# Two conformer layers and a hybrid block on one core: tile 3's output product and norm moved into the attention loop, four low weight parts subtracted by GpSimd, and other PSUM banks for the conv tiles

## What is computed

```
proj = h @ w_in[l]                       # a, g, zc, q, k, v, za, qi, ki, wi
y_conv = silu(LN(dwconv31(a * sigmoid(g)) + b)) * silu(zc)
score  = sum over 8 heads of relu(qi @ ki^T) * wi;  keep the top 132 keys of each query
y_attn = softmax(q @ k^T over the kept keys) @ v * silu(za)       # 8 heads of 64
h = LN(ALPHA * h + concat(y_conv, y_attn) @ w_out[l])
```

```
z = rmsnorm(x) @ w_in                    # q, k, v, gate_a, u, v_in, gate_b, g_merge
attention of 8 heads over 2 key/value heads, and a gated MLP that mixes positions
y = g0 * (attn @ w_proj_attn) + g1 * (gm @ w_proj_gmlp);  out = rmsnorm(x + y @ w_out)
```

## Time and profile before

| what | value |
|---|---|
| median of three runs | 1045.86 us |
| the profiled execution, its own time | 1047.51 us |
| its span on the core | 1045.7 us |
| TensorE matmul busy | 993.5 us (95%), 6452 instructions |
| VectorE busy | 653.0 us (62%) |
| ScalarE busy | 582.4 us (56%) |
| GpSimd busy | 198.7 us (19%) |
| DMA moved | 152.35 MB, mean 146 GB/s |

### The profile page before, as it was taken

One profiled execution on the slowest core, in us unless ns is written; L12 is line 12 of the kernel. 1 busy time (PEld: TensorE's weight loads), 2 busy tenths in 40 slices (PEclk: granted clock), 3 DMA queues, 4 the chain that ended last, 5 costly groups with the idle time before them and its releaser, 6 DMA issues.

```text
span 1045.7 us, 16515 instructions
## 1 busy us (share of the span) xinstructions
PE 993.5 (95%) x6452; PEld 838.9 (80%) x6452; DVE 653.0 (62%) x1423; ACT 582.4 (56%) x948; POOL 198.7 (19%) x238
## 2 busy tenths in 40 slices
PE   6999999998999899999999899899999899999997
PEld 6998988885577799898888676787888778878885
DVE  3899999876573489999987554637522333332422
ACT  6585881657444458588165834644656565554331
POOL 0100771113120210067111311224200000000001
PEclk9999999998999999999999899999999999999999
DMA  8776874844203768477474521857777535466662
GB/s 294 184 181 172 213 182 122 185 98 122 41 1 94 182 160 192 122 175 187 122 181 102 160 56 41 217 146 182 181 196 211 117 81 139 104 147 135 170 152 81
DMA packets 23820, 152.35 MB, mean 146 GB/s; under 512 B 2864, under 2 KB 3376, under 8 KB 6848
## 3 DMA queue, kind: packets, MB, share of 16 engines
q0 software_dynamic: 9648, 68.75, 35.4%
q1 hardware_dynamic: 14096, 82.55, 22.1%
HBM read 149.20 MB, written 2.10 MB: 145 GB/s over the span
## 4 chain that ended last, share of the span: by engine, by line
PE 79%; ACT 10%; DVE 5%; DMA 4%; issue 2%; POOL 0%; POOLq 0%; SPq 0%; DVEq 0%; ACTq 0%
PE psum_B L1274 20%; PE psum_A L1274 15%; PE psum_A L1307 8%; PE psum_B L1307 8%; PE psum_A L1456 5%; DMA w_lo<-in_weights 3%; PE psum_C L1349 2%; PE psum_A L1667 2%; PE psum_B L1667 2%; ACT w_hi L640 2%; PE psum_B L1410 2%; ACT w_lo L641 2%; PE psum_B L1456 2%; ACT exps L761 1%; DMA w_raw<-in_weights 1%
## 5 line engine op out<-in xcount | busy, mean ns | idle before, releaser
L1752 DVE SCALAR_TENSOR_TENSOR conv_acc<-u,vec,conv_acc 128x528 f32<-128x528 f32 (+1 forms) x240 | 172.4, 756 | 3.2
L1073 POOL DMA_DIRECT2D w_lo<-in_weights x67 | 59.3, 886 | 577.2 <-ACT w_lo L641 551.0
L1274 PE MATMUL psum_B<-x_hi,w_hi 128*128 128x264 f32 (+3 forms) x480 | 134.8, 321 | 5.3 <-DVE mlp_lo L2199 3.6
L640 ACT ACTIVATE w_hi<-w_raw 128x2048 fp32r<-128x2048 f32 (+2 forms) x87 | 129.8, 1493 | 12.7 <-DMA w_raw<-in_weights 12.2
L1274 PE MATMUL psum_B<-x_lo,w_hi 128*128 128x264 f32 (+3 forms) x480 | 132.6, 317 | 0.0
L1274 PE MATMUL psum_B<-x_hi,w_lo 128*128 128x264 f32 (+3 forms) x480 | 132.2, 316 | 0.0
L641 ACT ACTIVATE w_lo<-w_raw 128x2048 fp32r<-128x2048 f32 (+2 forms) x87 | 129.2, 1485 | 0.0
L1274 PE MATMUL psum_A<-x_hi,w_hi 128*128 128x264 f32 (+2 forms) x528 | 125.4, 291 | 3.4 <-DMA w_lo<-in_weights 2.2
L1274 PE MATMUL psum_A<-x_hi,w_lo 128*128 128x264 f32 (+2 forms) x528 | 122.7, 287 | 0.0
L1274 PE MATMUL psum_A<-x_lo,w_hi 128*128 128x264 f32 (+2 forms) x528 | 122.7, 286 | 0.0
L1274 PEld LDWEIGHTS psum_A<-x_hi,w_hi 128*128 128x128 f32 x528 | 87.5, 188 | 7.5 <-issue 5.6
(11 more groups left out here) (362 smaller groups left out, 2120.1 us busy)
## 6 DMA issues: line engine op xcount, KB each, us to landing
w_raw<-in_weights SPq DMA_DIRECT2D x67, 1024.0 KB, 5.3
w_lo<-in_weights POOLq DMA_DIRECT2D x65, 1024.0 KB, 8.4
x_first<-in_x_t SPq DMA_DIRECT2D x4, 528.0 KB, 7.1
h<-in_x SPq DMA_DIRECT2D x1, 2048.0 KB, 10.8
out<-h SPq DMA_DIRECT2D x4, 512.0 KB, 2.6
post_ln_g<-in_post_ln_g SPq DMA_DIRECT2D x2, 512.0 KB, 8.7
post_ln_b<-in_post_ln_b SPq DMA_DIRECT2D x2, 512.0 KB, 10.6
w_raw<-in_weights SPq DMA_DIRECT2D x2, 288.0 KB, 5.4
```

The lines of the kernel that those rows point to most:

```text
L640: act.activation(whi[n % RING][:, a:b], raw[n % RING][:, a:b], ACT.Copy)
L1073: pool.dma_start(wlo[n % RING][:, 0:width], io["weights"][n, :, 0:width], accum_op=ALU.add) \
L1274: mm = pe.matmul(ps[0:cols, i, 0:b - a], w[wp][:, kt, at:at + cols], x[xp][:, kt, a:b], start=(kt == 0 and wp + xp == 0), stop=(kt == KD - ...
L1752: got = dve.scalar_tensor_tensor(dst, src, w, dst, ALU.mult, ALU.add)
```

## The change

It does five things.

- Tile 3's second output half joins the first in both loops (`OUTPUT_AT`: items 34 and 36 in layer 0, 26 and 28 in layer 1). Its norm follows in the loop (`POST_AT`), tile 2's norm in layer 0 moves from item 34 to 32, and tile 4's conv halves are now made at item 38 (30) and behind the loop. Tile 3's rows are turned ahead of tile 4's last half.
- The low parts of the first two blocks behind each layer (`LO_BY_POOL`) are made by GpSimd: raw minus high part, in two halves of 1024 columns (`subtract_hi`), with a signal of its own, `pool_lo`. ScalarE writes only the high part of these.
- Conv tiles keep one bank for both turns and go round D, B, C. The affine step leaves `bank_holders` and stands behind the pair's second copy, directly ahead of its tanh.
- Rows that are turned use banks D and C; layer 0's second output product moves from bank B to A.
- The block's queries are made in halves over the four tiles (`query_half`), key/value and query products in single bank halves; tile 4's rows are turned behind the third key/value product.

```diff
 CONV_AT = {
-    0: ((0, 8, "D", "C"), (1, 10, "B", "C"), (2, 12, "D", "C"), (3, 14, "B", "C"), (4, 16, "D", "C")),
-    1: ((1, 8, "D", "C"), (2, 10, "B", "C"), (3, 12, "D", "C"), (4, 14, "B", "C")),
+    0: ((0, 8, "D"), (1, 10, "B"), (2, 12, "C"), (3, 14, "D"), (4, 16, "B")),
+    1: ((1, 8, "D"), (2, 10, "B"), (3, 12, "C"), (4, 14, "D")),
...
 OUTPUT_AT = {
-    0: ((17, 0, 0, "A"), (19, 0, 1, "B"), (22, 1, 0, "A"), (25, 1, 1, "B"), (27, 0, 2, "A"), (29, 1, 2, "A"),
-        (35, 0, 3, "A")),
-    1: ((17, 0, 1, "A"), (19, 0, 2, "B"), (21, 1, 1, "A"), (23, 1, 2, "A"), (27, 0, 3, "A")),
+    0: ((17, 0, 0, "A"), (19, 0, 1, "A"), (22, 1, 0, "A"), (25, 1, 1, "B"), (27, 0, 2, "A"), (29, 1, 2, "A"),
+        (34, 0, 3, "A"), (36, 1, 3, "A")),
+    1: ((17, 0, 1, "A"), (19, 0, 2, "B"), (21, 1, 1, "A"), (23, 1, 2, "A"), (26, 0, 3, "A"), (28, 1, 3, "A")),
...
 META_AT = ((14, "attn"), (14, "conv"))
-POST_AT = {0: ((0, 26), (1, 28), (2, 34)), 1: ((1, 22), (2, 26))}
-
-OUTPUT_CONV_AT = {0: (37, 39), 1: (29, 31)}
-OUTPUT_BANK = (("A", 1), ("C", 0))
-
-
-INPUT_BANK = {0: ("D", "B", "D", "D", "C"), 1: (None, "D", "B", "D", "C")}
+POST_AT = {0: ((0, 26), (1, 28), (2, 32), (3, 38)), 1: ((1, 22), (2, 26), (3, 30))}
+
+OUTPUT_CONV_AT = {0: 38, 1: 30}
+OUTPUT_BANK = (("A", 1), ("B", 1))
+
+
+INPUT_BANK = {0: ("D", "C", "D", "C", "D"), 1: (None, "D", "C", "D", "C")}
+
+
+KV_AND_Q = (("kv", 0), ("kv", 1), ("kv", 2), ("q", 0, 0), ("kv", 3), ("q", 1, 0), ("q", 2, 0), ("q", 3, 0),
+            ("q", 0, 1), ("q", 1, 1), ("q", 2, 1), ("q", 3, 1))
+KV_BANK = (("A", 0), ("B", 0), ("A", 1), ("B", 1))
+Q_BANK = (("A", 0), ("B", 0), ("A", 1), ("D", 0))
+
+LO_BY_POOL = {NUMBER[key] for key in ((1, "a", 0), (1, "g", 0), (2, "kv", 0), (2, "q", 0))}
...
                     act.activation(whi[n][:, a:b], raw[n][:, a:b], ACT.Copy).then_inc(hi_made.mark(("w", n)), 1)
+                    return
+                if n in LO_BY_POOL:
+                    for half in range(2):
+                        a, b = half * BLOCK // 2, (half + 1) * BLOCK // 2
+                        act.activation(whi[n % RING][:, a:b], raw[n % RING][:, a:b], ACT.Copy) \
+                            .then_inc(hi_made.mark(("w", n, half)), 1)
...
+                            conv_affine(l, op[1])
                             conv_tanh(l, op[1])
                         elif op[0] == "hi":
                             y_hi(l, *op[1:])
-                def bank_holders(i):
+                def gates(i):
                     for op in todo[i]:
                         if op[0] in ("za", "zc"):
                             gate_tanh(l, *op)
-                        elif op[0] == "affine":
-                            conv_affine(l, op[1])
                 for i in range(0, n, 2):
                     take_probs_t(l, i)
                     if i + 2 < n:
...
                         exps(l, i + 3)
-                    bank_holders(i)
+                    gates(i)
                     take_probs_t(l, i + 1)
                     woven(i)
-                    bank_holders(i + 1)
+                    gates(i + 1)
                     woven(i + 1)
                 after = NUMBER[(l + 1, "a" if l < DEPTH - 1 else "kv", 0)]
-                split_hi(after, 0)
                 y_hi(l, "attn", 4)
-                split_hi(after, 1)
+                split_hi(after)
                 if l < DEPTH - 1:
                     x_hi(l, 0)
-                x_hi(l, 1)
-                x_hi(l, 2)
-                split_hi(after + 1)
-                if l < DEPTH - 1:
+                    x_hi(l, 1)
+                    x_hi(l, 2)
+                    split_hi(after + 1)
                     x_hi(l, 3)
+                    split_hi(after + 2)
                     x_hi(l, 4)
+                else:
+                    x_hi(l, 1)
+                    x_hi(l, 2)
+                    split_hi(after + 1)
+                    x_hi(l, 3)
                     split_hi(after + 2)
-                else:
-                    squares(3, square)
-                    split_hi(after + 2)
+                    squares(4, square)
...
-                if (name, t) == ("kv", 1):
-                    x_hi(DEPTH - 1, 3)
-                    squares(4, square)
-                elif (name, t) == ("kv", 2):
+            for t in range(4):
+                take_rows("kv", t)
+                if t == 2:
                     x_hi(DEPTH - 1, 4)
                     split_hi(NUMBER[(2, "vin", 0)])
-                elif name == "q":
-                    next_blocks((2, "q", t))
+            split_hi(NUMBER[(2, "vin", 1)])
+            for t in range(4):
+                take_rows("q", t)
...
         def _(pool):
+            def subtract_hi(n):
+
+                for half in range(2):
+                    a, b = half * BLOCK // 2, (half + 1) * BLOCK // 2
+                    pool.wait_ge(hi_made.sem, hi_made.at(("w", n, half)))
+                    pool.tensor_tensor(wlo[n % RING][:, a:b], raw[n % RING][:, a:b], whi[n % RING][:, a:b].bitcast(F32),
+                                       ALU.subtract).then_inc(pool_lo.mark((n, half)), 1)
+
...
-                split_lo(after)
-                if l < DEPTH - 1:
-                    ln_deviation((l, "post", 3), 3, P)
-                    split_lo(after + 1)
-                    ln_deviation((l, "post", 4), 4, P)
-                    split_lo(after + 2)
-                else:
-                    ln_deviation((l, "post", 3), 3, P)
-                    split_lo(after + 1)
-                    input_deviation(3)
-                    split_lo(after + 2)
-                    ln_deviation((l, "post", 4), 4, P)
+                subtract_hi(after)
+                subtract_hi(after + 1)
+                ln_deviation((l, "post", 4), 4, P)
+                split_lo(after + 2)
+                if l == DEPTH - 1:
                     input_deviation(4)
...
                     pe.wait_ge(first_lo.sem, first_lo.at(n))
+                elif n in LO_BY_POOL:
+                    pe.wait_ge(pool_lo.sem, pool_lo.at((n, 1)))
                 elif n:
-                    pe.wait_ge(weights_lo[n % RING], 16 * (n // RING + (n % RING >= BY_DVE)))
+                    added = [m for m in range(n % RING, n + 1, RING) if m >= BY_DVE and m not in LO_BY_POOL]
+                    pe.wait_ge(weights_lo[n % RING], 16 * len(added))
...
-                    for name, c, turned in (("a", 0, 3), ("a", 1, 4), ("g", 0, None)):
+                    for name, c in (("a", 0), ("a", 1), ("g", 0)):
                         use = (l, name, c)
-                        ps = claim(use, next_buf("AB") if turned else "D")
+                        ps = claim(use, next_buf("AB") if name == "a" else "C")
                         w, cols, at = channel_weights(l, name, c)
                         first, second = pieces_of(l, name)
                         assert first[2] <= END[2]
                         product(ps, w, cols, at, (first,))
                         started.append((use, ps, w, cols, at, second))
-                        if turned:
-                            turn_rows(l - 1, turned)
+                        if c == 1:
+                            turn_rows(l - 1, 4)
                     x_ready(l - 1, 3)
...
-                ps = claim((l, "wo", 1, 3), "A", (0,))[:, 0, :]
-                output_half(l, 1, 0, 3, ps).then_inc(psum_full.mark((l, "wo", 1, 3, "conv")), 1)
+                output_conv(l, 1)
                 if l < DEPTH - 1:
                     turn_rows(l, 0)
                 turn_rows(l, 1)
+                if l == DEPTH - 1:
+                    turn_rows(l, 2)
                 output_attn(l, 0)
-                turn_rows(l, 2)
-                output_half(l, 1, 1, 3, ps).then_inc(psum_full.mark((l, "wo", 1, 3)), 1)
+                if l < DEPTH - 1:
+                    turn_rows(l, 2)
+                turn_rows(l, 3)
                 output_attn(l, 1)
...
-            for name, t in KV_AND_Q:
+            def query_half(t, half):
+
+                use = (2, "q", t)
+                buf, at = Q_BANK[t]
+                ps = (bank[buf][:, at:at + 1, :] if half else claim(use, buf, (at,)))[:, 0, :]
+                w = [part[:, :].rearrange("p (k c) -> p k c", k=4) for part in weights(NUMBER[(2, "q", 0)] + half)]
+                for kk in range(4):
+                    kt = 4 * half + kk
+                    for wp, xp in PASSES:
+                        mm = pe.matmul(ps, x[xp][:, kt, META + P * t:META + P * t + P], w[wp][:, kk, :],
+                                       start=(kt == 0 and wp + xp == 0), stop=(kt == KD - 1 and wp == 1))
+                if half:
+                    mm.then_inc(psum_full.mark(use), 1)
+
+            for name, t, *half in KV_AND_Q:
                 if name == "kv":
                     x_ready(1, t + 1)
-                    rows((2, "kv", t), NUMBER[(2, "kv", 0)], x, META + P * t, 1, 2 * P, 0, KD)
-                    if t in (1, 2):
-                        turn_rows(1, t + 2)
```

(29 more changed lines are left out.)

14 lines of the change are left out of this document (6 added, 8 removed).

## The result

The change takes 1036.57 us (median of four, 1035.59 to 1037.44) against 1045.32 us of the kernel before beside it: a ratio of 0.991, 95% interval 0.9889 to 0.993. Run once more, with a kernel before of its own beside it, it gave 0.9895 (0.9878 to 0.9913), so ratios from different sets of runs are compared to about 0.002. The forecast was 1037.6 us in a range of 1029.0 to 1042.5.

The account below looks back on a forecast made before the run. TensorE, busy 95% of the span, was taken as the bound. Layer 0's handoff -3.8, layer 1's -4.2 and conv -0.3 made -8.3 us, taking the median 1045.86 to 1037.6 us, range 1029 to 1042.5.

Parts of the forecast that it names:

- Low parts by GpSimd: Behind both layers: subtractions of 2.6 us each replace adding DMAs; TensorE's waits of 2.18, 2.80 and 2.51 us go.
- Z: End of a layer's last probabilities-times-values product, where the conv half behind it starts; 330.9 us in layer 0.
- The copies of the last turns: End of both loops: TensorE waits 0.83 us for ScalarE's probability copies, two per layer, 1.66 us a layer.
- Layer 0's handoff: From layer 0 to layer 1: waits removed less new waits, including 1.0 us for tile 4's norm; net -3.8 us.
- Layer 1's handoff: From layer 1 to the block behind: -9.9 us of waits and slow products, +5.8 of new waits; -4.2 unrounded.
- The conv tiles: Both attention loops: the chain runs outside TensorE, so waits change names and keep their sum; net -0.6 and +0.3 us.
- the two slow stretches: Conv tiles in both loops, 243 to 252 and 588 to 596 us, at 1.2 GHz: both forecast to stay.
- The conv waits: Rival, chance 0.14 at full or half size: loop conv waits of 10.1 us go, giving 1021.0, or 1029 at half.
- Tile 4's norm is late next: Behind each layer: tile 4's norm chain leaves TensorE idle 2.3 us in layer 1 and 1.0 in layer 0.
- rival 2: Both handoffs: tile 4's norm replaces what goes, 3 us more each; 1047.2 at worst, 1042 likely; chance 0.12.
- the affine steps come onto TensorE's path: Rival, conv tiles: 1.37 us at each of nine tiles, 12.3 in all, giving 1049.9 us; chance 0.05.
- Rival 4: Handoffs: low parts in time, but TensorE waits for x_lo as before; nothing moves, 1045.9 us; chance 0.03.

Follow-up runs that it names:

- change_again: The unedited change run once more, with its own kernel before beside it: 1035.82 us, ratio 0.9895.
- sub_alone: The kernel before with only the low parts of the two blocks behind each layer subtracted by GpSimd: 1046.67 us, ratio 0.9996.
- low_by_dma: The change with the low parts of the two blocks behind each layer made by ScalarE copy and adding DMA again: 1048.02 us, ratio 1.0004.
- parted: The change with tile 3's second output product and tile 4's first conv half one item later in both layers: 1039.73 us, ratio 0.9925.
- parted_layer0: The change with the half products moved between the turns of probabilities in layer 0's loop alone: 1035.28 us, ratio 0.9883.
- y_late: The change with VectorE's gate of conv tiles 1 to 4 one item later, their high and low parts two later: 1037.34 us, ratio 0.9905.
- conv_alone: The kernel before with only the conv part (one bank, later affine step, layer 0's second output product in bank A): 1048.16 us, ratio 1.0007.
- best_y: The change with later gates, layer 0's half products between turns, layer 1's tile 4 rows turned behind the first query half: 1035.7 us, ratio 0.9885.

## Why the prediction was right, point by point

**The sum.** Predicted -8.3 us, measured -10.1 by the profiled spans and -8.75 by the medians; beside change_again the medians differ by 11.5. That 8.75 comes so near to 8.3 is in part luck: by their stretches the two handoffs brought 11.0 us, where the forecast had 8.0. Of the terms:

- *Low parts by GpSimd.* The three waits went, as said, and no wait for a low part came. One subtraction took 2.37 us, not the 2.6 taken from twice the 512-column row, and the last ended at Z+14.6, not Z+16.1. The Trainium skill's floor of some 2.5 cycles an element (GPSIMD Engine Reference, Instruction dispatch), gives an estimate of 2.13 us. The measured 2.37 lies halfway between that and 2.6. What the prediction had not said is that this part brings nothing measurable alone (sub_alone) and that without it the new order brings nothing either (low_by_dma).
- *The copies of the last turns* wait 0.88 and 0.83 us in each layer: 3.4 us against 3.3 said. parted and parted_layer0 show that in layer 0 they, and 0.3 us more, can be had for nothing, in layer 1 not.
- *Layer 0's handoff*: -4.3 against -3.8. Tile 4's rows wait 0.7 us, not 1.0.
- *Layer 1's handoff*: -6.7 against -4.2, the largest miss. The mechanism was right: the wait for h_normed stands where it was forecast, and VectorE's norm step is held until about the end of the last subtraction. Its size failed at "GpSimd's subtraction of the second block runs until Z+16.1: 2.2 us": it holds the step by 0.46, the wait is 1.07 instead of 2.3, tile 2's rows wait 0.52 instead of 0.65, tile 3's not at all instead of 0.25, and the clock stays at 2.4 GHz where 0.9 us was set aside. These make 1.2 + 0.1 + 0.25 + 0.9 = 2.5. That tile 3's rows did not wait hangs on the 0.24 us by which VectorE came first; y_late, where the lead was 0.05 us, waits 1.83 us there.
- *The conv tiles.* Their waits kept their sum, 10.1 and 10.4 us, under new names, as said from the chain, and conv_alone shows it. The forecast for the two loops, -0.6 and +0.3, came the other way round, +1.2 and -0.8. One profile hardly tells this (two of the change differ by 0.9 in loop 0). Of the two slow stretches both stay, the one in layer 1 shorter. Why VectorE's gate was on that chain I had right; that behind it stood a DMA for the attention half's low part I had not seen. It showed as a wait named "issue" at layer 0's second output product, 0.5 us before and 1.7 in the change (there the DMA landed at 271.42 us and the matmul started at 271.51).

**The rivals.** The conv waits did not go. Tile 4's norm is late next, with 1.07 and 0.7 us instead of the 2.3 and 1.0 of the forecast; the 3 us more in each layer of rival 2 did not come. That the affine steps come onto TensorE's path is out: conv_alone is at 1.0007 (at most 1.002), against 1.012 for 12.3 us. Rival 4 is out too: no wait for x_lo is left. My own expectations failed more often than the prediction. At sub_alone, parted, y_late and best_y it was each time one thing: a wait was taken away and the next one in line was not priced. At low_by_dma I priced the waits too high.

## What to carry to other kernels

Two parts of a change that each bring nothing can bring 1% together, if each removes what holds the other up; undo them one by one before crediting either. A wait that is moved is to be priced by what is queued behind it on its own engine, not only by who waits for the result. A low part that was subtracted by a quiet GpSimd was ready 5.9 us after ScalarE started on its block (338.24 to 344.12 us in the change), where the copies and the adding DMA took 14.1 (337.39 to 351.50 in low_by_dma); look for every such DMA on the path, also for those that stand behind other waits.
